# A second mixer whose head tiles are copied by ScalarE and scaled by GpSimd instead of VectorE

## What is computed

```python
hn = rms_norm(h, norms[i, 1])
cq, ckv, kidx, widx, dq, dk, dv = split_cols(hn @ od_w_in[j], OD_WIDTHS)
o_c = dsa_mixer(cq, ckv, kidx, widx, ...)
o_d = diff_attention(dq, dk, dv, ...)
mix = jnp.concatenate([o_c, o_d], axis=-1) @ od_w_out[j]
...
# dsa_mixer, per block of 128 queries
cq, ckv = rms_norm(c_q, q_norm), rms_norm(c_kv, kv_norm)
score = einsum(relu(q_idx . k_idx), w_h)       # index scores of every visible key
_, idx = lax.top_k(score, 128)                 # 128 keys kept per query
s = softmax over the kept keys; ctx = s @ c_sel; out = ctx @ w_uv
# diff_attention, per block: two softmaxes a[0], a[1] per head
attn = a[:, :, 0] - lam * a[:, :, 1];  o = attn @ v;  o = rms_norm(o) * (1 - lam_init)
```

## Time and profile before

| | |
|---|---|
| time, median of 3 runs | 1954.14 us (1954.06 to 1954.20) |
| the profiled execution's own time | 1956.61 us |
| its span | 1954.8 us |
| granted TensorE clock over the span | 0.994 |
| TensorE busy | 1917.9 us, 98% |
| VectorE busy | 1028.6 us, 53% |
| ScalarE busy | 636.4 us, 33% |
| GpSimd busy | 288.2 us, 15% |
| second mixer, first chunk to the first chunk after it | 1281 to 1522 us of the span |

### The profile page before, as it was taken

One profiled execution on the slowest core, in us unless ns is written; L12 is line 12 of the kernel. 1 busy time (PEld: TensorE's weight loads), 2 busy tenths in 40 slices (PEclk: granted clock), 3 DMA queues, 4 the chain that ended last, 5 costly groups with the idle time before them and its releaser, 6 DMA issues.

```text
span 1954.8 us, 24237 instructions
## 1 busy us (share of the span) xinstructions
PE 1917.9 (98%) x8980; PEld 1546.9 (79%) x8980; DVE 1028.6 (53%) x1502; ACT 636.4 (33%) x959; POOL 288.2 (15%) x221
## 2 busy tenths in 40 slices
PE   8999999999999999999999999999989999999997
PEld 6888888777888888887888888877657888888885
DVE  5444477664645442347544542369984644442345
ACT  5332222244323222224322322234573423222222
POOL 2000001311300000224000000162243200000225
PEclk9999999999999999999999999999999999999998
DMA  5323223322222323322322233331101323322321
GB/s 174 106 86 107 97 98 102 88 87 82 88 94 87 111 92 107 108 76 88 104 91 93 88 114 99 97 116 65 54 1 44 108 86 98 105 97 97 108 75 54
DMA packets 56730, 179.59 MB, mean 92 GB/s; under 512 B 12144, under 2 KB 12144, under 8 KB 56656
## 3 DMA queue, kind: packets, MB, share of 16 engines
q1 hardware_dynamic: 54656, 173.69, 27.6%
q0 software_dynamic: 928, 3.02, 0.5%
q10 hardware_dynamic: 1088, 2.10, 0.3%
HBM read 175.04 MB, written 3.15 MB: 91 GB/s over the span
## 4 chain that ended last, share of the span: by engine, by line
PE 91%; DVE 4%; POOL 2%; ACT 1%; issue 1%; DMA 0%; POOLq 0%; SPq 0%; DVEq 0%; ACTq 0%
PE ps L1799 57%; PE ps L1816 25%; PE ps L2244 2%; PE ps L1906 1%; POOL sumsq L1276 1%; POOL square L1274 1%; PE ps L2144 1%; PE ps L2162 1%; DVE sm L1004 0%; PE ps L2193 0%; DVE t L504 0%; PE ps L2177 0%; PE ps L1957 0%; PE ps L1826 0%; PE ps L2003 0%
## 5 line engine op out<-in xcount | busy, mean ns | idle before, releaser
L1799 PE MATMUL ps<-x_hi,w_hi 128*128 128x512 f32 x1728 | 683.1, 395 | 10.7 <-ACT w_hi L357 7.4
L1799 PE MATMUL ps<-x_lo,w_hi 128*128 128x512 f32 x1728 | 675.3, 391 | 0.0
L1799 PE MATMUL ps<-x_hi,w_lo 128*128 128x512 f32 x1728 | 675.3, 391 | 0.0
L365 DVE TENSOR_TENSOR w_lo<-raw,w_hi 128x1024 fp32r<-128x1024 f32 x310 | 396.9, 1296 | 409.2 <-ACT w_hi L357 403.3
L357 ACT ACTIVATE w_hi<-raw 128x1024 fp32r<-128x1024 f32 x322 | 332.3, 1050 | 341.1 <-PE ps L1816 293.6
L1799 PEld LDWEIGHTS ps<-x_hi,w_hi 128*128 128x128 f32 x1728 | 326.0, 189 | 85.0 <-ACT w_hi L357 7.4
L1799 PEld LDWEIGHTS ps<-x_lo,w_hi 128*128 128x128 f32 x1728 | 326.2, 189 | 68.8 <-issue 2.4
L1799 PEld LDWEIGHTS ps<-x_hi,w_lo 128*128 128x128 f32 x1728 | 326.0, 189 | 68.8 <-DVE w_lo L365 0.8
L1816 PE MATMUL ps<-act_hi,w_hi 128*128 (+1 forms) x720 | 280.3, 389 | 0.0
L1816 PE MATMUL ps<-act_hi,w_lo 128*128 (+1 forms) x720 | 280.1, 389 | 0.0
L1816 PE MATMUL ps<-act_lo,w_hi 128*128 (+1 forms) x720 | 280.1, 389 | 0.0
(11 more groups left out here) (360 smaller groups left out, 1322.0 us busy)
## 6 DMA issues: line engine op xcount, KB each, us to landing
raw<-in_weights SPq DMA_DIRECT2D x322, 512.0 KB, 3.4
h<-in_xT ACTq DMA_DIRECT2D x4, 512.0 KB, 6.8
out<-result SPq DMA_DIRECT2D x4, 512.0 KB, 3.0
p_raw<-in_pT POOLq DMA_DIRECT2D x2, 512.0 KB, 4.0
scratch_u<-u_sc SPq DMA_DIRECT2D x1, 512.0 KB, 6.6
u_grp<-scratch_u SPq DMA_DIRECT2D x1, 512.0 KB, 4.1
scratch_y<-y_grp SPq DMA_DIRECT2D x2, 256.0 KB, 3.1
y_ch<-scratch_y SPq DMA_DIRECT2D x1, 512.0 KB, 3.6
```

The source lines that it names most:

```text
L365: dve.tensor_tensor(w_lo[:, slot], raw[:, slot], w_hi[:, slot].bitcast(F32), SUB)\
L1799: last = pe.matmul(ps[:, bank], w[:, slot, k], x[:, k], start=(k == 0 and part == 0), stop=(k == KD - 1 and part == 2))
```

## The change

On VectorE the scaling of the twelve head tiles and of the three latents goes. ScalarE copies the twelve tiles unscaled out of their banks (`evict`), in front of the `split_hi` that waits for the same chunk; GpSimd multiplies each in place by `rstd`, in front of one of its twelve `split_lo`, and scales the latents behind chunk 9's. The bank is free for TensorE when ScalarE has copied (`z_raw`), the tile is ready when GpSimd has scaled (`z_ready`). Both tables of selection steps are new: 44 steps stand in `SELECTS` (35 before) and 10 in `GROUP_SELECTS` (19 before).

```diff
-SELECTS = {4: 1, 6: 1, 7: 5, 8: 5, 9: 4, 10: 4, 11: 4, 12: 3, 13: 4, 14: 4}
-GROUP_SELECTS = {12: 2, 13: 2, 14: 2, 15: 2, 16: 1, 17: 1, 18: 1, 19: 1, 20: 1, 22: 1, 23: 1, 24: 1,
-                 25: 1, 26: 1, 27: 1}
+SELECTS = {4: 2, 5: 1, 6: 3, 7: 6, 8: 5, 9: 5, 10: 4, 11: 5, 12: 4, 13: 4, 14: 4, 15: 1}
+GROUP_SELECTS = {12: 1, 13: 1, 14: 1, 15: 1, 16: 1, 17: 1, 18: 1, 20: 1, 22: 1, 24: 1}
...
-            def latents():
-                dve.wait_ge(od_s["rstd"], 2)
-                dve.wait_ge(od_s["qidx_done"], 2)
-                for i, x in enumerate((cq[:, 0], cq[:, 1], ckv[:])):
-                    dve.tensor_tensor(x, x, (std, sumsq)[i // 2][:], MULT)\
-                       .then_inc(od_s["latent"], 1)
...
             for j in range(OD_IN):
-                scale(j)
+                if j < 4:
+                    scale(j)
...
-                if j == 6:
-                    latents()
...
-            pool.wait_ge(z_ready, z_base(5) + 3)
+            pool.wait_ge(z_ready, z_base(5) + 4)
...
             pool.wait_ge(split_ready, first + AHEAD + DVE_AHEAD)
-            for j in range(DVE_AHEAD, OD_IN + 2):
-                split_lo(pool, first, AHEAD + j)
+            pool.wait_ge(rstd_ready, 6)
+            for j in range(4, OD_IN):
+                pool.wait_ge(od_s["z_raw"], j - 3)
+                hh, kind = divmod(j - 4, 3)
+                dst = (dq, dk, dv)[kind][:, hh % 2]
+                pool.tensor_tensor(dst, dst, rstd[:], MULT).then_inc(z_ready, 1)
+                split_lo(pool, first, AHEAD + DVE_AHEAD + j - 4)
+                if j == 9:
+                    pool.wait_ge(od_s["rstd"], 2)
+                    pool.wait_ge(od_s["qidx_done"], 2)
+                    for i, x in enumerate((cq[:, 0], cq[:, 1], ckv[:])):
+                        pool.tensor_tensor(x, x, (std, sumsq)[i // 2][:], MULT)\
+                            .then_inc(od_s["latent"], 1)
...
+            def evict(j):
+                hh, kind = divmod(j - 4, 3)
+                act.wait_ge(chunk_used, first + j + 1)
+                if hh >= 2 and kind < 2:
+                    act.wait_ge(od_s["scores"], 2 * NQ * (hh - 1))
+                if hh >= 2 and kind == 2:
+                    act.wait_ge(od_s["dv_turned"], hh - 1)
+                act.activation((dq, dk, dv)[kind][:, hh % 2], ps[:, od_bank(j)], ACT.Copy)\
+                   .then_inc(od_s["z_raw"], 1)
+
             for j in range(OD_IN):
+                if j >= 4:
+                    evict(j)
                 split_hi(act, first, AHEAD + 2 + j)
...
             for j in range(OD_IN):
-                if j >= 4:
-                    pe.wait_ge(z_ready, zb + (j - 3 if j < 6 else j - 1))
+                if j in (4, 5):
+                    pe.wait_ge(z_ready, zb + j - 3)
+                if j >= 6:
+                    pe.wait_ge(od_s["z_raw"], j - 5)
```

More of the change, by code:

```diff
@@ L331, in encoder @@
             "w_loaded", "w_gained", "sq_step", "ssq", "std", "rstd", "latent", "lam", "const",
-            "qidx_done", "qidx_read", "weight_done", "weight_read", "index_done", "relu_done",
+            "z_raw", "qidx_done", "qidx_read", "weight_done", "weight_read", "index_done", "relu_done",
             "index_step", "sel_step", "dv_turned", "dv_read", "scores", "masked", "exp", "mix_step",
@@ L899, in scale @@
                     dsts = [(kidx[0:HD], half), (kidx[HD:P], half), (widx[rows], rows)]
[L900 to L906, removed]
                 scale_tile(dve, 5, first, j, od_bank(j), dsts)
```

## The result

The changed kernel took 1961.44 us (median of 7 runs, 1959.16 to 1962.61) against 1954.19 for the kernel before (7 runs, 1952.67 to 1957.34): a ratio of 1.0031, 95% interval 1.0020 to 1.0042. It is slower, by 6.1 us by the ratio (3.9 to 8.2) and 7.2 by the medians. The profiled execution took 1960.01 us.

The account below looks back on a forecast made before the run. TensorE was taken to bound the kernel while the chunks run. TensorE 4.9 us late at turn(11), less 4.4 us given back, made +0.5 us on the 1954.14 us median: 1954.6 us, range 1948.7 to 1959.2.

Parts of the forecast that it names:

- What bounds the kernel: Second mixer: TensorE is full while the chunks run, so work taken from VectorE there buys nothing by itself.
- The prize: Behind the chunks: TensorE's waits of 6.3 us, 3.9 for GpSimd's normalising and 2.4 for VectorE.
- VectorE's own sum, 2.4 us more: VectorE up to mix(11): 13.1 us of steps added, 6.7 of scalings and 4.0 of latents gone.
- I take three quarters, 6.2 ... Net 3.9: VectorE waiting on GpSimd up to mix(11): 8.3 us of collisions cut to 6.2, less 2.3 of old ones.
- The four places: Expected VectorE collisions with GpSimd: first combine 0.9, lam_value 1.5, behind chunk 9 2.9, behind chunk 13 3.0 us.
- ScalarE and the route of a tile, priced at nothing: ScalarE's twelve copies, 7.2 us in all, and the tiles' later readiness were claimed to cost nothing.
- The slack of 1.4 us: Between mix(11) ending at 1406.7 and TensorE's turn(11) at 1408.10; mix(11) 6.3 later makes TensorE 4.9 late.
- The give-back: Groups 16 to 27, with five fewer steps: 4.4 us back, lower bound 2, upper 6.3.
- The fourth: Sign of being right: TensorE's waits in the old stretch of groups 16 to 27 fall from 6.3 to about 2 us.
- The first: Rival: collisions stay as rare as before, TensorE loses nothing, 4.4 to 6.3 us come back; 1947.8 to 1949.7 us; chance 0.27.
- The second: Rival: the lock catches most of the twelve mixes, 7 us more at mix(11); 1961.6 us, half of it 1958.1; chance 0.17.
- The third: Rival: freed time is filled with steps, ScalarE uncovered behind; small early loss, small late gain; 1953 to 1956 us; chance 0.10.

Follow-up runs that it names:

- x10_no_reads_old: Changed kernel with the old selection tables, GpSimd's scalings, latents and twelve splits replaced by writes of a constant: 1954.01 us, ratio 0.9992.
- x8_nine_less: Changed kernel with the old SELECTS and new GROUP_SELECTS, nine late selection steps left out altogether: 1955.97 us, ratio 0.9999.
- x6_scale_only: Kernel before with only the twelve tiles' way changed (ScalarE copies, GpSimd scales), latents on VectorE, old tables: 1958.68 us, ratio 1.0011.
- x9_no_reads: Changed kernel with its own tables, GpSimd's scalings, latents and twelve splits replaced by writes of a constant: 1951.99 us, ratio 0.9985.
- x1_old_tables: Changed kernel with both tables of selection steps as before (35 and 19 steps): 1956.71 us, ratio 1.0007.
- x5_fill_idle: Changed kernel with 38 early steps, three more than the old tables, placed in chunks 4 to 6: 1957.23 us, ratio 1.0008.
- x3_write_only: Changed kernel with GpSimd's fifteen products replaced by writes of a constant to a free tile, splits kept: 1957.70 us, ratio 1.0016.
- x11_latents_fill: Kernel before with latents scaled on GpSimd behind chunk 9's split and three more steps in chunks 4 to 6: 1959.70 us, ratio 1.0018.
- x4_latents_back: Changed kernel with the three latents scaled on VectorE again in chunk 6: 1959.38 us, ratio 1.0023.

## Why the prediction was wrong

**What bounds the kernel** was right, and x10_no_reads_old shows it: 13 us of idle VectorE bought nothing against the kernel before by themselves. The prize, waits behind group 16, was real too.

**VectorE's own sum, 2.4 us more, was right.** Without GpSimd's reads and with the new tables `mix(11)` is 1.3 us later than before: 2.4, less the 2.4 us of old collisions, less 1.4 at the first `combine`, plus 1.9 of idle time and 0.7 of short waits.

**The failing step is the size of the collisions, "I take three quarters, 6.2 ... Net 3.9".** Measured over the plain lengths of the same operations:

| place | as laid | measured |
|---|---|---|
| first `combine`, more than before | 0.9 | 0.4 |
| `lam_value` and the combine beside it | 1.5 | 1.8 |
| behind chunk 9 | 2.9 | 3.3 (L973 1.4, L957 0.8, L958 0.8, L1003 0.3) |
| behind chunk 13 | 3.0 | 2.9 (L958 0.8, L962 2.1) |
| a `mix`, L1003 at 1382.19 | not seen | 1.8 |
| old ones that go | -2.3 | -2.4 |

Net 7.8 instead of 3.9, and 2.4 + 7.8 = 10.2 against 10.1 measured. The four places came to 8.4 us against the 8.3 laid, but that agreement is in part luck: 1.4 of it is the one-input L973, which was not in the sum, and `L1023` of `mix(3)`, which was, lost nothing. What was in the sum came to 7.0. So of the 3.9 us missing, 1.8 are a mix behind chunk 12, which the overlay did not see; 1.4 are L973, left out; and 0.8 are the discount of a quarter, which was not earned (7.0 for 6.2; the old collisions give 0.1 back). Two smaller errors lie inside. GpSimd's product of two full tiles was priced at 1.03 us, from a row in which both inputs are the same tile; the trace of before also had a sum of two different tiles, L1336 at 1312.74, with 1.27 us, and 1.27 to 1.31 is what L1328 takes. And L973, priced as "about 1 us in the finishing steps" by the wider form of the Trainium skill's rule and left out of the sum, took 1.4 over its length.

**ScalarE and the route of a tile, priced at nothing**, cost little, but not nothing. The first copy stands in front of ScalarE's `relu`, so the first `combine` starts 0.4 us later from the mixer's head (21.8 for 21.4); VectorE's idle time before masks fell by as much, which hides it in the sum. For the last `dv` tile TensorE waited 1.5 us for GpSimd, where it had waited 0.6 for VectorE, but 0.4 us for `mix(11)` after it: `mix(11)` still decided, as forecast.

**The slack of 1.4 us was right**: 10.1 late at `mix(11)`, 8.7 at `turn(11)`.

**The give-back was too high: 4.4 forecast, 2.6 measured** (8.7 late at `turn(11)`, 6.2 at the last update); 3.2 by x8_nine_less against x6_scale_only. I let a third of the 6.3 us of waits remain, which would leave 4.2 and not the 4.4 that I wrote. Of VectorE's 2.4 us 0.6 are left, but of GpSimd's 3.9 still 2.9: that wait hangs on the chain of exponentials, reciprocal and normalising, not on the steps. 6.3 - 3.5 = 2.8 us could come back.

Right numbers in the same sum give 10.2 - 1.4 - 2.6 = +6.2 us. The ratio says 6.1, the medians 7.2, the traces 6.2. The stretch at half clock behind the wait of 2.5 us (1359.1 to 1362.5 us) was not in the sum and did not need to be: VectorE held the path there, with 0.2 us of idle time up to `mix(11)`, all of it before that stretch.

**The signs.** Of the signs of being right three came: unit 12's mask starts at 1412.4, after 1408; TensorE waits for masks inside the chunks; two-input operations take 1 to 2 us and more beside GpSimd's. The fourth did not: the late waits fell from 6.3 to 3.5 us, not to about 2.

**The rivals.** The first (collisions rare, 1947.8 to 1949.7 us) asks what the kernel does without them: x9_no_reads takes 1952.0, a gain of 3.1 us and not of 4.4 to 6.3. The second named the time, 1961.6, but only in part the place; in the changed kernel the mixes lose 2.1 us (1.8 and 0.3), and most of the loss is in finishing steps and combines. Its mechanism is seen in x1_old_tables, where four operations of the mixes take 1.08 to 2.80 us. The third is out: TensorE loses 8.7 us up to `turn(11)`.

## What to carry to other kernels

Work moved from VectorE to GpSimd is not off VectorE: of 10.7 us, 7.8 came back as stalls. Lay GpSimd's new stays over VectorE's operations with SBUF inputs, one-input ones too, take the sum of the overlaps at full, and only then fill the room that is left. And room on an engine that does not bound is worth nothing until something late is put into it; what that returned here, 2.6 us, is about what TensorE had waited for that engine (2.4), not the whole wait of the stretch (6.3). Three steps put into idle time (x5_fill_idle) returned nothing that could be measured.

## What the runs showed of the hardware that I had not expected

- GpSimd's float32 operation on two inputs of 128x512 takes 1.03 us where both inputs are the same tile and 1.27 to 1.31 where they are two (L1332 and L1336 of the kernel before, L1328 of the changed one).
- A one-input `TENSOR_SCALAR` of VectorE in SBUF, plain 0.35 us, stood 1.78 us beside GpSimd's split (after) and 2.69 us across a split and a pure write (x3_write_only); two-input ones kept their plain length inside pure writes (x9_no_reads).
- TensorE's granted clock fell to half for 3.4 us in the changed kernel, behind a wait of 2.5 us, and in x11_latents_fill for 13.7 us in all: 10.2 of it behind waits of 2.1 to 2.3 us, the other 3.4 behind waits of 0.4 and 0.6 only. In x4_latents_back a wait of 1.5 us was followed by none. Where the full engine is the one that decides, such a wait may be charged twice; in the changed kernel it was not, as VectorE decided.
